# Seven of the first tile's output-projection products placed between the steps of the RWKV state scan

## What is computed

```python
mixed = jnp.concatenate([y_rwkv, y_pool, y_fox], axis=-1)
x = x + g1 * (mixed @ w_out[l])
h = rms_norm(x, norm2[l]) * (1.0 + sc2) + sh2
x = x + g2 * moe_ffn(h, router_w[l], router_b[l], moe_w_gu[l], moe_b_gu[l],
                     moe_w_down[l], moe_b_down[l])
```

```python
state = (state * w_t[:, :, None, :]
         + sa[..., None] * (kk_t * a_t)[:, :, None, :]
         + v_t[..., None] * k_t[:, :, None, :])
```

## Time and profile before

| | us |
|---|---|
| median of 3 runs | 1544.02 (1543.7 to 1544.58) |
| the profiled execution, its own time | 1545.55 |
| its span | 1543.8 |
| PE busy | 1483.1 (96%) |
| DVE busy | 1376.1 (89%) |
| ACT busy | 1015.2 (66%) |
| the scan's steps 0 to 6, first product to the last new state | 279.61 to 287.64 |
| tiles 0 and 1 of the output projection | 288.32 to 320.53 |
| tiles 2 and 3 | 321.04 to 346.18 |
| first expert's products | from 373.14 |

### The profile page before, as it was taken

The page is one execution under the profiler, slowest core; times in us unless marked ns, Lnnn a source line. Parts: engine busy times, 40 slices in busy tenths (PEclk is TensorE's granted clock), DMA queues, the critical chain, the costliest instruction groups (busy, mean ns, idle before and its releaser), DMA issues.

```text
span 1543.8 us, 22843 instructions
## 1 busy us (share of the span) xinstructions
PE 1483.1 (96%) x8567; PEld 1175.4 (76%) x8567; DVE 1376.1 (89%) x1070; ACT 1015.2 (66%) x839; POOL 230.9 (15%) x240
## 2 busy tenths in 40 slices
PE   5999899997999999999999999999999999999996
PEld 3786677564788888888888888888888888888873
DVE  7979765588999999999999999999999999999987
ACT  4335433245577777777777777777777777777772
POOL 4454020000111111111111111111111111110060
PEclk9999999897999999999999999999999999999998
DMA  9778400227899999999999999999999999999992
GB/s 381 289 263 330 151 30 17 60 83 281 316 382 393 387 383 389 389 385 396 401 383 382 384 395 380 397 389 387 393 391 386 384 391 389 375 391 393 376 384 96
DMA packets 90601, 507.73 MB, mean 329 GB/s; under 512 B 12440, under 2 KB 13768, under 8 KB 39216
## 3 DMA queue, kind: packets, MB, share of 16 engines
q1 hardware_dynamic: 75712, 454.66, 75.0%
q0 software_dynamic: 9104, 34.08, 6.2%
q10 hardware_dynamic: 5728, 18.18, 2.9%
HBM read 478.04 MB, written 28.85 MB: 328 GB/s over the span
## 4 chain that ended last, share of the span: by engine, by line
PE 89%; DVE 5%; DMA 2%; ACT 1%; issue 1%; POOL 1%; ACTq 0%; DVEq 0%; POOLq 0%
PE ps L2488 66%; PE ps L1294 2%; PE ps L1413 2%; PE ps L2467 2%; PE ps L1416 2%; PE ps L1419 2%; PE ps L2503 2%; PE ps L1328 1%; PE ps L2370 1%; PE ps L1430 1%; DMA R<-y_rows,row_of 1%; PE ps L2477 1%; PE ps L1526 1%; PE ps L1383 1%; DVE R L1079 1%
## 5 line engine op out<-in xcount | busy, mean ns | idle before, releaser
L1716 DVE TENSOR_TENSOR w_lo<-w_raw,w_hi 128x2048 fp32r<-128x2048 f32 x384 | 865.3, 2288 | 60.7 <-ACT w_hi L1710 55.3
L1710 ACT ACTIVATE w_hi<-w_raw 128x2048 fp32r<-128x2048 f32 x384 | 736.4, 1920 | 271.9 <-PE ps L2488 271.7
L2488 PE MATMUL ps<-w_hi,xTh 128*128 128x512 f32 x1024 | 407.7, 398 | 1.9 <-DVE xTl L2200 1.9
L2488 PE MATMUL ps<-w_lo,xTh 128*128 128x512 f32 x1024 | 400.8, 391 | 0.0
L2488 PE MATMUL ps<-w_hi,xTl 128*128 128x512 f32 x1024 | 275.3, 391 | 0.0
L2488 PEld LDWEIGHTS ps<-w_hi,xTh 128*128 128x128 f32 x1024 | 193.6, 189 | 49.0 <-issue 7.5
L2488 PEld LDWEIGHTS ps<-w_hi,xTl 128*128 128x128 f32 x1024 | 193.3, 189 | 40.4
L2488 PEld LDWEIGHTS ps<-w_lo,xTh 128*128 128x128 f32 x1024 | 193.7, 189 | 38.3
L2488 PE MATMUL ps<-w_hi,aTh 128*128 128x512 f32 x512 | 202.4, 395 | 0.0
L2488 PE MATMUL ps<-w_lo,aTh 128*128 128x512 f32 x512 | 199.4, 389 | 0.0
L1758 POOL TENSOR_TENSOR carried<-iotaE 128x1 f32<-128x1 f32 x64 | 27.9, 436 | 990.3 <-PE ps L2467 868.3
(11 more groups left out here) (443 smaller groups left out, 1571.1 us busy)
## 6 DMA issues: line engine op xcount, KB each, us to landing
w_raw<-in_moe_w_gu SPq DMA_DIRECT2D x256, 1024.0 KB, 7.0
w_raw<-in_moe_w_down SPq DMA_DIRECT2D x128, 1024.0 KB, 7.7
y_rows<-R ACTq DMA_DIRECT2D x30, 512.0 KB, 7.8
Wt<-in_ada_w SPq DMA_DIRECT2D x10, 1024.0 KB, 4.9
y_rows<-Wt POOLq DMA_DIRECT2D x1, 8704.0 KB, 25.4
Wt<-in_ada_w SPq DMA_DIRECT2D x16, 512.0 KB, 10.7
Wt<-in_w_in SPq DMA_DIRECT2D x4, 2048.0 KB, 9.6
R<-in_ada_w SPq DMA_DIRECT2D x6, 1024.0 KB, 7.9
```

The lines of the kernel that those rows point to most:

```text
L1710: nc.scalar.activation(w_hi[:, at[-1] % HI_SLOTS, :], w_raw[:, at[-1] % RAW_SLOTS, :], ACT.Copy).then_inc(hi_rdy, 1)
L1716: nc.vector.tensor_tensor(w_lo[:, s, :], w_raw[:, s, :], w_hi[:, at[-1] % HI_SLOTS, :].bitcast(F32), ALU.subtract).then_inc(lo_rdy, 1)
L2488: ins = mm(ps[:, bank0 + c, :], x[:, k, :], w[:, 512 * (banks * i + c):512 * (banks * i + c) + 512], start=(first and i == 0 and x is xh a ...
```

## The change

Seven of tile 0's twelve products of blocks 2 to 7 are made in the scan: one behind each of the steps 0 to 6, after the step's output products and ahead of the next step's wait for `st_new`. Three more stand behind chunk 7, the last two between the two sums, and none behind the second sums. The products, their banks and their order of summing are the same; tile 1 is as before. The wait for the `w_out` blocks and for the reader of the pooling heads' bank now stands ahead of the scan.

```diff
             def project(t, parts):
 
-                if t == 0 and parts[0] == 2:
-                    pe.wait_ge(wout_in, 48)
-                    read_by(pe, ("pm", CT - 1))
                 for m in parts:
...
             pe.wait_ge(fox_oe, 4)
             pe.wait_ge(st_zero, 1)
+            pe.wait_ge(wout_in, 48)
+            read_by(pe, ("pm", CT - 1))
+            first_rows = [(m, c) for m in range(2, KT) for c in range(2)]
+
+            def project_first(n):
+                m, c = first_rows[n]
+                mm(ps[:, c, :], mixed[m][:, 0:P], w_out_sb[:, m, 512 * c:512 * c + 512], start=(m == 2), stop=False)
+
             for c in range(NC):
                 if c:
                     pe.wait_ge(st_new, c)
...
+                if c < NC - 1:
+                    project_first(c)
             ins.then_inc(y_mm, 1)
-            project(0, (2,))
+            for n in range(NC - 1, NC + 2):
+                project_first(n)
             for ct in range(CT):
                 pe.wait_ge(y_sum, ct + 1)
                 mm(ps[:, 6 + ct, :], blockones[:], lnY[:, ct, :], start=True, stop=True).then_inc(mean_mm, 1)
-            project(0, (3,))
+            for n in range(NC + 2, len(first_rows)):
+                project_first(n)
             for ct in range(CT):
                 pe.wait_ge(y_sq, ct + 1)
                 mm(ps[:, 4 + ct, :], blockones[:], lnS[:, ct, :], start=True, stop=True).then_inc(mean_mm, 1)
-            project(0, (4, 5, 6, 7))
             project(1, (2, 3, 4, 5, 6, 7))
```

## The result

The changed kernel took 1546.38 us (median of 18 runs, 1544.31 to 1551.32), the kernel before on the same chips 1543.59 us (18 runs, 1539.78 to 1547.35). The ratio is 1.0024, 95% interval [1.0016, 1.0031]: slower by 3.7 us, between 2.5 and 4.8 (the two medians alone differ by 2.8). Forecast were 1547.0 us and a sum of 3.0 us more. The change of 0.24% lies just past the 0.2% that the prediction took as its bound, where I had given "same" 0.53 and "slower" 0.42.

The account below looks back on a forecast made before the run. TensorE, 89% of the chain of waits, was taken to bound the kernel. A first sum 3.5 us later was to make tile 3 3.0 us later; 1544.02 + 3.0 = 1547.0 us, range 1543.5 to 1550.0.

Parts of the forecast that it names:

- a sum of 3.0 us more: At tile 3's start: 3.0 us later, waiting for DVE's second residual, passed on to the end.
- a step is 0.47 + 0.86 + 0.08 = 1.41 us: Scan step at full clock: sixteen small-product rows 0.47, one large product 0.86, change between sizes 0.08 us.
- The 0.08 for the change of sizes: In each scan step: 0.08 us for the change between small and large products.
- The rise of the clock: In the scan: full clock from 284.3, between ends of 283.0 and 285.6, with the scan starting at 279.61.
- The norm was to end at most 5 us later: Sign at the norm behind the scan: prediction wrong if it ends less than 1.5 or more than 5 us later.
- the experts' stretch was to keep its length within 1.5 us: Sign behind tile 3: prediction wrong if the experts' stretch changes its length by more than 1.5 us.
- another start at 373.20: Half-clock stretch at 373.20: could come out shorter by up to 1.3 us, not part of the sum.
- a clock that stays at half through the scan: Rival in the scan: half clock throughout, 11.6 us late at the end, 1555.6 us; chance 0.07.
- a clock that falls in the second gap: Rival before tile 2: half clock behind the second gap, 3.6 to 5.1 us at the end, 1548.4 us; chance 0.14.
- an early clock: Rival in the scan: clock up early or size switch free, 0.5 to 1.1 us late, 1544.8 us; chance 0.12.
- a gain: Rival at TensorE's waits: filling them makes the kernel faster, 1541 us at best; chance 0.07 with all else unseen.
- my two readings: Clock in the scan: released by busy time, 0.5 to 1.1 us late; or by work in the array, 3.0 us.

Follow-up runs that it names:

- filled gap: The changed kernel with two more products, their result unread, in the gap ahead of the wait for `rw_out`; ratio to the kernel before 1.0030.
- early biases: The changed kernel with DVE's four instructions on the experts' biases and the norm's scale moved into the scan and the waits for the sums; ratio to before 1.0011.
- the second pair of profiles: The kernel before and the changed kernel, each run and profiled once more without further edits; ratios to before 1.0000 and 1.0034.
- products behind three steps: The changed kernel with large products only behind the scan's steps 4, 5 and 6; ratio to before 1.0012.
- late loads: The kernel before, and the changed one, with SP's eleven small router and bias loads issued only after the scan's first new state; ratios to before 0.9996 and 1.0023.
- the early scan: The kernel before, its scan waiting for ACT's read of the last `GH` bank only at chunk 5; ratio to before 1.0000.
- the short way to the sum: The changed kernel with two of the three products between scan and first sums moved behind the second sums; ratio to before 1.0022.

## Why the prediction was right, and where it was off

The direction and the way were right. I had the scan grow since a product adds more than it covers; two new gaps behind it, both for DVE; the first covering a fall of the clock; and tile 3 late by the norm's delay less 0.5 us. The profile shows each: 5.08 us of delay at the first sum and 4.64 at tile 3, gaps of 2.43 (2.6 forecast) and 1.09 (1.5), and the clock down from 311.9 to 315.3, from just behind the gap on. The filled gap showed that this fall costs nothing, and the early biases that DVE's stream is one of the two ways by which the delay arrives.

The term that was mis-sized is the step: "a step is 0.47 + 0.86 + 0.08 = 1.41 us". It measured 1.66. The small products take 0.61 us in place of the 0.47 that I took from other 64x64 products; why, no run shows. The 0.08 for the change of sizes is 0.19, the length of a weight load that nothing hides behind products this short. Both are 0.25 us a step and 1.3 us over the five steps at full clock. At half clock the step was 3.06 instead of 2.76. I had read the 0.08 from the one place where the scan now ends and large products begin, and spread over four rows at a changing clock it was too small to be read well. The rise of the clock fit: 4.7 us after the scan's start was taken, 4.4 came. So the delay was 5.1 instead of 3.5 us at the first sum, and 4.6 instead of 3.0 at tile 3.

Two of the signs by which I would have called the prediction wrong are there. The norm was to end at most 5 us later: from the scan's start it ends 5.08 us later, and 5.58 in the second pair of profiles, which is the step once more. And the experts' stretch was to keep its length within 1.5 us: it is shorter by 2.1 us, and by 3.7 in the second pair; but since it moves by 2.2 us between the two executions of the kernel before, one pair of profiles can't decide this sign. I had allowed up to 1.3 for another start at 373.20 and left it out of the sum, and had nothing for the clock being up when the experts begin. So in the first pair of profiles two errors pull against each other, a delay that is larger than forecast and a stretch behind it that is shorter; that the time came out so near is in part luck.

At the end 3.7 us [2.5, 4.8] arrived in the first comparison and 5.2 [3.2, 7.4] in the second, with 4.6 to 5.1 at tile 3 in the profiles. That the median of 1546.38 is near the forecast 1547.0 owes something, too, to the kernel before having been 0.43 us faster in the 18 runs than in the first three; by the ratio the sum of 3.0 is 0.7 too small.

The rival of a clock that stays at half through the scan did not come (1555.6). That of a clock that falls in the second gap did not come either in the changed kernel, but it did in two of its variants, just where the first gap was closed: it needed the first gap to leave the clock up, as it said. The rival of an early clock did not come, and the early biases show that a gain had to get past DVE. Of my two readings of the Trainium skill's account of the clock ("TensorE: Matmul & The Clock Gate", Part 1: matmul activity releases the throttle), neither fits all profiles. The scan of the kernel before stood at 0.50 for 8 us with TensorE recorded busy for 7.74 of them, against the first. The second agrees with the rise at 281.2 in the changed kernel; but with products behind three steps, with late loads and with the early scan, the clock rose under the small products alone.

## What to carry to other kernels

A filler in a loop between two engines is worth the wait that it covers and costs what it sticks out: here it covered 0.23 us, filled 1.05, and stuck out of every one of seven steps. Before work is moved ahead of a chain's start, look where that chain's end is waited for, and not only at the first wait: here the slack of 4.3 us at `rw_out` was real, while DVE's stream behind it had 0.5. And in short loops, a large product has to be priced with the load of its stationary operand: behind the small products here it took 0.19 us more than its columns, as long as such a load.

## What the runs showed of the hardware

- A 128x128 product behind 64x64 products took 0.19 to 0.20 us more than its columns at full clock and 0.28 to 0.29 at half, for both of its widths. At full clock that is the length of one load of its stationary operand. In rows of large products there is nothing of the kind (0.43 us a row).
- Idle gaps of 2.43 us and 2.79 us, begun at full clock, were followed by PEclk 0.50 for 3.4 us in every profile that has one; it fell 0.1 to 1.5 us behind the gap's end. Gaps of 1.09 to 1.20 us left it at 1.00. At one place ahead of the scan a gap of 1.51 us was followed by 0.50 in the kernel before, and one of 1.52 in the kernel with the short way to the sum was not.
- The scan's small products alone left the clock at 0.50 for more than 8 us in the two profiles of the kernel before. Under the same work it rose 8.1 and 8.5 us after the scan's start with late loads and with the early scan, and after 3.5 us, at 280.3, in the kernel with three products. What decides this stays open.
- A gap that no semaphore explains, ahead of the last GH products, was 2.18 to 2.21 or 1.90 us and became 1.63 when eleven small loads were moved away from it.
